# The first norm's sum of squares: added up over the tiles on GpSimd, and summed over the partitions by one product inside the queries' products

## What is computed

```python
def rms_norm(x, gain):
    xf = x.astype(jnp.float32)
    y = xf * lax.rsqrt(jnp.mean(xf * xf, axis=-1, keepdims=True) + NORM_EPS)
    return (y * gain.astype(jnp.float32)).astype(x.dtype)
...
        h = rms_norm(x, g_pre_mix[i])
        proj = h @ w_in[i]
        sb_q, sb_k, sb_v, q_lat, kv_lat, k_rope = jnp.split(proj, split_at, axis=-1)
```

## Time and profile before

| | |
|---|---|
| median of 3 runs | 954.4 us (953.57 to 956.45) |
| the profiled execution's own time | 951.65 us |
| its span in the profile | 949.8 us |
| TensorE busy | 797.9 us, 84% of the span |
| VectorE, ScalarE, GpSimd busy | 349.2, 326.7, 144.4 us |
| mean DMA rate | 314 GB/s |

### The profile page before, as it was taken

One profiled execution on the slowest core, in us unless ns is written; L12 is line 12 of the kernel. 1 busy time (PEld: TensorE's weight loads), 2 busy tenths in 40 slices (PEclk: granted clock), 3 DMA queues, 4 the chain that ended last, 5 costly groups with the idle time before them and its releaser, 6 DMA issues.

```text
span 949.8 us, 12498 instructions
## 1 busy us (share of the span) xinstructions
PE 797.9 (84%) x5234; PEld 527.7 (56%) x5234; DVE 349.2 (37%) x734; ACT 326.7 (34%) x655; POOL 144.4 (15%) x152
## 2 busy tenths in 40 slices
PE   9999999999999999999899997567665675756765
PEld 7985578999998867778777443123221221211212
DVE  6746766666675454397503011010010100101002
ACT  5665656666665476354622100001000000000012
POOL 0011031555531051183100000000000000000000
PEclk9999999999999999999999999788798888798868
DMA  9955972644435566635367999999999999999995
GB/s 358 396 209 221 430 293 90 265 177 178 178 123 186 198 260 265 221 134 211 144 273 276 407 424 429 429 428 429 426 426 428 428 428 427 426 431 425 428 431 209
DMA packets 24111, 297.95 MB, mean 314 GB/s; under 512 B 2673, under 2 KB 3057, under 8 KB 5489
## 3 DMA queue, kind: packets, MB, share of 16 engines
q1 hardware_dynamic: 24048, 297.09, 76.9%
HBM read 296.03 MB, written 1.05 MB: 313 GB/s over the span
## 4 chain that ended last, share of the span: by engine, by line
PE 57%; DMA 32%; ACT 4%; DVE 4%; POOL 1%; issue 1%; POOLq 0%; DVEq 0%; ACTq 0%
PE ps L107 56%; DMA ring<-in_exps 32%; ACT ar L116 1%; POOL ar L125 1%; ACT fr L116 1%; PE ps L110 1%; DVE ar L125 1%; ACT ar L113 1%; ACT sq L113 1%; DVE misc L148 0%; DVE fr L125 0%; DVE yT L125 0%; DVE yT L129 0%; DVE rb L136 0%; DVE hT L133 0%
## 5 line engine op out<-in xcount | busy, mean ns | idle before, releaser
L107 PE MATMUL ps<-ring,sq 128*32 128x512 f32 x944 | 138.8, 724 | 74.3 <-DMA ring<-in_exps 74.0
L107 PE MATMUL ps<-fr 128*128 128x256 f32 (+1 forms) x956 | 163.3, 323 | 1.1 <-DVE fr L125 1.1
L107 PEld LDWEIGHTS ps<-fr 128*128 128x128 f32 x956 | 140.1, 190 | 16.9 <-issue 1.3
L107 PE MATMUL ps<-ring,ar 128*32 128x512 f32 (+3 forms) x792 | 105.4, 623 | 41.8 <-DMA ring<-in_exps 36.6
L107 PEld LDWEIGHTS ps<-ring,sq 128*32 128x32 f32 x944 | 28.8, 121 | 172.3 <-DMA ring<-in_exps 117.7
L125 DVE TENSOR_TENSOR ar<-ar,ps 128x512 f32<-128x512 f32 x9 | 6.2, 687 | 256.7 <-PE ps L107 256.7
L125 DVE TENSOR_TENSOR fr<-ring,fr 128x512 fp32r<-128x512 f32 (+1 forms) x96 | 77.8, 829 | 49.5 <-ACT fr L116 49.1
L125 POOL TENSOR_TENSOR ar<-ar 128x256 f32<-128x256 f32 (+2 forms) x51 | 34.8, 683 | 391.3 <-DVE ar L125 364.1
L116 ACT ACTIVATE ar<-ps 128x512 f32<-128x512 f32 (+5 forms) x49 | 27.5, 566 | 166.1 <-PE ps L110 146.2
L107 PEld LDWEIGHTS ps<-ring,ar 128*32 128x32 f32 (+1 forms) x792 | 27.9, 120 | 100.8 <-DMA ring<-in_exps 53.1
L116 ACT ACTIVATE fr<-ring 128x512 fp32r<-128x512 f32 (+1 forms) x114 | 66.7, 625 | 26.8 <-PE ps L107 23.6
(11 more groups left out here) (187 smaller groups left out, 950.0 us busy)
## 6 DMA issues: line engine op xcount, KB each, us to landing
ring<-in_exps SPq DMA_DIRECT2D x86, 2048.0 KB, 30.9
ring<-in_modw SPq DMA_DIRECT2D x12, 2048.0 KB, 8.8
ring<-in_wup SPq DMA_DIRECT2D x11, 2048.0 KB, 9.1
ring<-in_wdown SPq DMA_DIRECT2D x5, 2048.0 KB, 7.7
ar<-in_exps SPq DMA_DIRECT2D x5, 2048.0 KB, 12.9
ring<-in_win SPq DMA_DIRECT2D x4, 2048.0 KB, 7.6
ring<-in_exps SPq DMA_DIRECT2D x6, 1024.0 KB, 7.7
ring<-in_wo SPq DMA_DIRECT2D x2, 2048.0 KB, 9.9
```

Of the source, the lines that this page charges most:

```text
L107: return Issue(self.e and self.e.matmul(o, l, r, start=start, stop=stop, skip_group_check=True))
```

## The change

The squares are no longer summed tile by tile on TensorE. GpSimd adds the 8 tiles of `sq` up in four operations: three of 512 columns (tiles 0 and 1 plus tiles 2 and 3; tiles 4 and 5 plus 6 and 7; the two results) and one of 256. One product by the full block of ones then sums over the partitions; it stands behind step k = 5 of the queries' products, and TensorE waits there for the last of the four operations. The sums reach bank 0 without the factor of 32, so the copy out of PSUM and the second product are gone. The root moves on ScalarE: it now stands ahead of the six roundings of the keys' weights, and waits there for the product. On GpSimd the additions stand ahead of `spread_cond`.

```diff
@@ tensor
                 t.then_inc(pe_in, "q", k)
-            pe.wait_ge(landed["con"]["all"])
-            column_sums(0, [(tile(sq, k), act_in["sq", k // 4]) for k in range(8)]).then_inc(pe_in, "sums")
+                if k == 5:
+                    pe.wait_ge(landed["con"]["all"], pool_in["squares"])
+                    pe.matmul(half(0, 1), ones, tile(sq, 0), True, True).then_inc(pe_in, "total")
...
-                if k == 0:
-                    pe.wait_ge(act_in["sums"])
-                    pe.matmul(half(0, 1), ones, sd[:, 0, :], True, True).then_inc(pe_in, "total")
@@ scalar
             act.activation(silu_c, col("c", 0, 8), ACT.Silu).then_inc(act_mod, "silu")
+            act.wait_ge(pe_in["total"], dve_in["eps"])
+            row_root(sd[:, 0, :], half(0, 1), 1024).then_inc(act_in, "root")
             for k in range(6):
                 if k == 5:
                     act.wait_ge(dve_in["pos"])
                 rounded("k", k, act_in)
-            act.wait_ge(pe_in["sums"])
-            act.copy(sd[:, 0, :], half(0, 0)).then_inc(act_in, "sums")
-            act.wait_ge(pe_in["total"], dve_in["eps"])
-            row_root(sd[:, 0, :], half(0, 1), 32 * 1024).then_inc(act_in, "root")
@@ gpsimd
+            for i in range(2):
+                a, b = (sq[:, 1024 * i + 512 * n:1024 * i + 512 * n + 512] for n in range(2))
+                pool.wait_ge(t, act_in["sq", i])
+                t = pool.tensor_tensor(a, a, b, ALU.add).then_inc(pool_in, "half", i)
+            pool.wait_ge(t)
+            t = pool.tensor_tensor(sq[:, 0:512], sq[:, 0:512], sq[:, 1024:1536], ALU.add).then_inc(pool_in, "pairs")
+            pool.wait_ge(t)
+            t = pool.tensor_tensor(tile(sq, 0), tile(sq, 0), tile(sq, 1), ALU.add).then_inc(pool_in, "squares")
             t = spread_cond(0, t)
```

## The result

The change makes the kernel slower by about 3 us. The median of 15 runs is 957.05 us (953.45 to 958.81) against 954.19 us (950.54 to 956.89) of the kernel before: the medians lie 2.86 us apart, a quotient of 1.0030. The ratio of the two kernels, which is not worked out as this quotient, is 1.0037, or 3.5 us, with a 95% interval from 1.0022 to 1.0052 (2.1 to 5.0 us) that holds both. The ratios in the table of experiments are of this second kind. The forecast was 954.5 us in a range up to 956.6, and no measurable change.

What follows compares the result with a forecast made beforehand. TensorE was taken to bound the start, arriving weights the end. Its saving of 1.09 us and a 1.22 us wait for VectorE summed to +0.13 us: 954.5 us in median terms, range 952.4 to 956.6.

Steps and rivals of the forecast that it cites:

- What bounds the kernel, and the saving: Start of the kernel: TensorE is the chain from 9 to 34 us and does 1.09 us less; later, arriving weights.
- GpSimd's additions in time for TensorE: Queries' products: squares added before TensorE asks at 16.09 us, 1.2 us to spare with waits, no new TensorE wait.
- VectorE's operations with one tensor "as free": VectorE beside GpSimd's additions: only two-input operations take turns, scalings are undisturbed; angles begin 1.51 us late.
- What that does to TensorE: Keys' products: begin at 19.97 us, then TensorE waits 1.22 us for VectorE's first lo (0.77 by the smaller delay).
- the cover of 0.8 us: Queries' products: h 4 ready at 11.81 us, needed by TensorE at 12.62, so VectorE's lateness is covered there.
- The carry of 1 to 1: From the start to the end: a gain or loss near the start reaches the end in full.
- ScalarE's order: ScalarE: root from about 16.73 us, then six roundings to 20.6, hidden by over 3 us before VectorE uses them.
- Rival 1: VectorE is not held up where it hurts, so TensorE's saving stands whole: -1.09 us, 953.3 us; chance 0.12.
- Rival 3: Squares late at TensorE's wait through slow GpSimd additions: about +2, 956.5 us; a 6 us first call, 20.9; chance 0.05.

Runs made afterwards that it cites:

- e2: The changed kernel without GpSimd's four additions, the product taking only the first tile's squares and the root dividing by 128; ratio to the kernel before 0.9989.
- e6: The changed kernel with GpSimd's second addition waiting for VectorE's last scaling of hT; ratio to the kernel before 1.0013.
- e8: The changed kernel with the second addition behind VectorE's last scaling and the second table of angles behind lo of step 2; ratio to the kernel before 1.0011.
- e5: The changed kernel with the scalings of tiles 4 to 7 by the constant 1.0 instead of the column of gains; run once, no ratio, scores at 36.77 us.
- e4: The changed kernel with the root put back behind ScalarE's six roundings; ratio to the kernel before 1.0030.
- e3: The kernel before with six more products by ones ahead of the sums, results unread; ratio to the kernel before 1.0039.
- e1: The kernel before with GpSimd's four additions put in, written to a free buffer, and a wait at the sums; ratio to the kernel before 1.0030.

## Why the prediction was wrong

**What bounds the kernel, and the saving.** Right. TensorE saves 1.09 us; e2 gives 1.15 once its early start and its wait are taken off. From the first wait for weights to the end the time is the same within 1.5 us in all traces but one, as the prediction said.

**GpSimd's additions in time for TensorE.** Right in effect: 1.27, 1.52, 1.26 and 0.73 where 1.30 and 0.6 were put, with `total` at 17.37 directly behind step 5. But that was in part because TensorE was late itself: the additions end at 15.69, so at the 16.09 of the forecast 0.4 us would have been to spare, not 1.2. e6 and e8, which begin the second addition about 1 us later than the changed kernel, ran into the wait.

**VectorE's operations with one tensor "as free".** This is the step that failed. I had seen only pairs of two-input operations take turns, and took the others as not concerned without a row for it. (In rows 8 the 0.832 is set against a form that reads PSUM. The right row is the shortest of its own form, 0.483 in the same stage, and the reading stands.) In the changed kernel they are: two of 1.35 and 1.42 in the scalings and parts of two more, 3.89 us for 1.13. e5 shows it for a scaling by a constant, e6 for a CAST and for the angles' short operations. Of VectorE's lateness at the angles, 17.60 - 13.95 = 3.65 us, the first `x_lo` make 0.95, the scalings with their gaps 16.16 - 12.34 - 1.05 = 2.77, the input's later landing 0.84, and 0.92 is taken in by the wait for `pos` that was there. I had 1.51: in its sum the scalings had nothing, and the second `x_lo`, which met no addition in the end, had 1.52 with the wait ahead of them. So of the 2.14 us that were missing, the failed step makes 2.77 - 1.52 = 1.25 and the later landing 0.84.

**What that does to TensorE.** The mechanism was right and the size was off by that amount. The keys begin at 21.07, not 19.97, because `h` 4 is there at 13.69, not 11.81: the cover of 0.8 us that I named was gone. The third pass then comes at 24.40, 3.33 behind, not 1.05: a wait of 2.28 where I had 1.22. Together 1.10 + 1.06 = 2.16 over the forecast's +0.13, which gives +2.29; the scores show +2.39.

**The input's landing.** It wasn't in the forecast at all. In the kernel before VectorE waits for `pos`, and TensorE's products up to the keys' wait for nothing of VectorE's. Its third trace has a landing at 7.18 instead of 6.47 and scores 0.29 us later, but 0.28 of this is a break near 9.3 us, where the queries' weights landed late. In the changed kernel that slack is used up: with landings at 7.13 (e4), 7.31, 7.37 and 8.11 TensorE's third pass comes at 24.23, 24.40, 24.46 and 25.20, the same 17.1 us behind each. The four scalings take 3.89 or 3.90 in all of these.

**The carry of 1 to 1.** Wrong, and too small. Up to 580 us the delay grew from 2.39 to 3.80 in the first trace, to 6.9 and 7.7 in the others, counted from the kernel before's first trace. What is added are stretches of TensorE at the lower clock: around 150 us in all three, around 25 and 525 in the second and third. The one around 480 is no addition, the kernel before has one at 475. The one at 25 stands right behind the wait of 2.04 us, and no trace of the kernel before has it; but the changed kernel's first trace and e4 have the same wait and no slow stretch behind it. The two that have it waited longer in the queries' products ahead (1.46 and 1.49 us, against 0.64 and 0.94). That TensorE's waits bring it is likely and not shown. The later stretches come with a bare delay too (e3), so they need no additions. They don't grow with the delay: e1, at 1.51 us, has none, less than the kernel before; e5, at 3.12 us, has one. What decides their number stays open. So does their share in the measured 2.9 to 3.5 us: the delay at the scores of the first trace alone, 2.39 us, is a ratio of 1.0025, and lies inside the interval of 1.0022 to 1.0052.

**ScalarE's order.** Right in effect (e4). The root ran at 19.52 and not at 16.73, because the roundings `x_hi` ahead of it waited for the scalings that were held up; the first rounding of the keys' weights was still ready 3.1 us before VectorE came to it.

**The rivals.** Rival 1, no hold-up, was wrong by the x_lo rows alone. Rival 3 named the other side, but for GpSimd being late at TensorE; in the changed kernel GpSimd was in time, and VectorE was late behind it. The 20.9 us that it gives for a late first addition have the whole 6 us added at the end, though 0.85 us of them would have gone into the idle time between the first two additions; 20.0 is nearer. The first addition took 1.27 us, so the case didn't arise.

## What to carry to other kernels

An engine that is idle in the profile is not free if its operations hold those of a busy one up. Ahead of work moved to GpSimd, list VectorE's operations in the same stretch, and take each that reads and writes SBUF, one-tensor ones too, as waiting for the GpSimd operation that it meets; then look who waits for VectorE. Check how late inputs may land: a change that uses up a slack also lets every later landing through. Where a long chain passes through short waits, a shift of 1 to 3 us at its start can change TensorE's granted clock far behind it, so one trace doesn't show what a shift is worth. Count the stretches of lower clock in each trace before two traces are compared.

## What the runs showed of the hardware

- A VectorE TENSOR_SCALAR of 128x256 float32 on SBUF takes 0.346 us alone and up to 1.42 beside a GpSimd addition of 128x512; by a constant 0.281 and 1.36; a CAST of 64x256 0.33 and 1.24. It ends about 0.15 us behind the addition that it met. The Trainium skill (SBUF — State Buffer, section "SBUF: two separate sides") gives the lock against VectorE operations in a 2-port mode or with two SBUF inputs. The prediction used only the second half of this, and the scalings fit the first. Groups of the kernel before, by form (busy us, mean ns of one):

```profile
L129 DVE TENSOR_SCALAR ar<-ar,misc 128x256 f32<-128x256 f32 x8 | 2.8, 347 | 0.0
L129 DVE TENSOR_SCALAR ar<-ar,misc 128x128 f32<-128x128 f32 x8 | 2.3, 283 | 0.1
L122 DVE COPY ar<-ps 128x512 f32<-128x512 f32 x5 | 3.5, 690 | 2.0 <-PE ps L107 2.0
L122 DVE COPY ar<-ps 128x256 f32<-128x256 f32 x8 | 3.3, 415 | 2.9 <-PE ps L110 2.9
```

- A scaling by a column takes 64 ns more for 128 more columns, 0.5 ns each, and a copy out of PSUM 275 ns more for 256, 1.1 ns each. So the scaling on SBUF runs at about twice the rate of the copy. That this is the 2-port mode, and that the mode is why the scaling was held up, is argued from this and not shown.
- A VectorE operation that reads PSUM wasn't held up. In the kernel before two copies of 128x512 took 0.69 us each beside four two-input operations of GpSimd on end, as long as the copies of this size in the rows above:

```profile
129.78 0.69 DVE L122 COPY yT<-ps 128x512 f32<-128x512 f32 x1 [0.47 <-ACT sq L113]
131.79 0.69 DVE L122 COPY yT<-ps 128x512 f32<-128x512 f32 x1 [1.31 <-ACT sq L113]
```

```profile
127.23 5.97 POOL L125 TENSOR_TENSOR fr<-ring,fr 128x512 fp32r<-128x512 f32 x4 [14.15 <-ACT fr L116]
```

- It works the other way too: the addition of 128x512 that begins among four `x_lo` in e6, at 13.15, takes 2.29 us, and 1.27 alone.
- The same program can have other stretches of lower clock in another execution: none in the changed kernel's first trace from 24 to 34 us, 0.83 in the second.
